# First attention: unscaled outputs divided by GpSimd with inverse sums sent through DRAM, and first steps placed between the picking rounds

## The chip, the cores and the metric

One core of one Trainium2 chip runs the whole program. The metric is the time of one execution on the device in microseconds (us). The engines are TensorE (PE in the profile; PEld is its weight load), VectorE (DVE), ScalarE (ACT), GpSimd (POOL) and SyncE (SP, which here only starts transfers). Each runs its own instruction stream in order, and the streams meet at semaphores.

## The reference, cut to what matters

The program computes two transformer blocks on 512 tokens of width 1024 in float32. The change touches the first mixer of the first block, an attention over the keys that an index score picks: 16 query heads of width 64, 4 key heads, 128 picked keys per query, causal.

```python
def block(i):                       # 128 queries
    ...
    s = einsum('bqhd,bsd->bqhs', iq_b, ik) * IDX_DIM ** -0.5
    score = einsum('bqh,bqhs->bqs', iw_b, relu(s))       # 8 index heads
    score = where(causal, score, -inf)
    _, sel = lax.top_k(score, top_k)                     # top_k = min(256, L // 4) = 128
    ...
    logits = einsum('bqgrd,bqkgd->bqgrk', q_b, k_sel) * A_HEAD_DIM ** -0.5
    logits = where(valid, logits, -inf)
    p = softmax(logits)
    o = einsum('bqgrk,bqkgd->bqgrd', p, v_sel)
...
mix = o @ w_o                       # then layer norm, MLP, and the other mixers
```

## The kernel before

Tokens are tiled in T = 4 tiles of 128. Every large product is done in three passes of fp32r matmuls: each operand is split into a high part (ACT's copy, `high`, line 1243) and a low part (the difference, `low`, DVE's line 1859), and high x high, high x low and low x high are summed. Weights come in numbered chunks of 1 MB: SP fetches chunk i into one of three `raw` buffers as soon as the low part of chunk i - 3 is made. For a few chunks (`pool_low` = 5, 6, 7, 8) POOL makes the low part (line 2772). Chunks 7 and 8 belong to the second half of the query projection, 9 to 12 to the output projection (`a_w_o`), 13 on to the MLP. Chunks 11 and 12 use slots that overlap buffers of the attention (`lent`), so ACT waits for the attention's last output before it writes them.

Before the attention, DVE picks the keys. For token tiles 1, 2 and 3 it runs 16 rounds each of `max` (the 8 largest, line 2214) and `match_replace` (line 2216), and then turns the result into a bias of 0 or -1e30 (line 2220). This runs as a job beside the projections of k, v and q on PE. Tile 0 needs no picking.

The attention (`attend` with key "A") is written out as a software pipeline of 32 units. Unit u is the pair of heads j = u // 4 and the query tile t = u % 4, and covers 128(t+1) keys; each unit has two score blocks i = 2u and 2u + 1, one per head. Step u of the pipeline does on

- PE: the scores of unit u (line 818); the transposes of the probabilities of unit u - 3 (line 827, `LAG`), and every second step the products with v (line 843), half 0 or 1 of the outputs of a pair, two units later still;
- DVE: for both blocks the biased scores and their maximum in one instruction (line 2097); for unit u - 1 the reciprocal of the row sum (line 2110) and, for t = 2 and 3, the scaling of the probabilities by it (line 2114); the copy of one transposed block out of its bank (line 2126); at the end of a pair the low part `xl` of the output (line 2229);
- ACT: both exponentials with row sums (line 1399); the copy of the other transposed block (line 1343); at the end of a pair the high part `xh` (line 1473);
- POOL: for t = 0 and 1 the scaling (line 2761).

PE's transposes therefore wait for scaled probabilities. PE's eight PSUM banks are handed out in turn, and each `take` waits until the bank's last reader is done. When the second query half is projected (`gemm_tok(("q", 1), ...)`), POOL rotates it (`rotary`, lines 2746 to 2750, with `gb` as scratch), and after step 3 PE transposes it (line 540, 16 transposes in four banks) and ACT copies it (line 1248).

After the attention `first_half` runs chunk 9 and then chunk 10 against the outputs of head pairs 0 to 3 (lines 720 to 722), and `cross` runs chunks 11 and 12 against pairs 4 to 7.

## Time and profile before

| | |
|---|---|
| median of 3 runs | 1945.25 us (1945.1 to 1946.36) |
| profiled execution | 1947.47 us, of which the span is 1945.5 us |
| PE busy | 1869.9 us (96%) |
| DVE busy | 1184.5 us (61%) |
| ACT busy | 734.1 us (38%) |
| POOL busy | 136.5 us (7%) |

The span in 40 slices of 48.6 us; a digit is the busy share in tenths, and PEclk is the granted clock in tenths. The first attention lies in the third to fifth slice.

```profile
PE   9989999999999999999999999789899899999997
DVE  4989676555556676577544546766775554333437
ACT  4447343232223434544222223535554352222221
POOL 0343000000000151000000000000230000000000
PEclk9989999999999999999999999989999899999998
```

Busy times are sums of instructions and say nothing of who waits for whom. A matmul's end is modelled, so short waits of PE are seen best from the starts of its groups. In the timeline a row is a start, a duration, the engine, the line, the operation with its operands and the number of merged instructions, and in brackets the idle time before it and what ended it.

### The profile page before, as it was taken

What the parts mean: (1) busy time and instruction counts of PE and PEld (TensorE: products, weight loads), DVE (VectorE), ACT (ScalarE), POOL (GpSimd) and SP (SyncE); (2) the same over time, 40 slices, a digit from 0 to 9 for tenths busy, and PEclk for the clock granted to TensorE, in tenths of its full rate; (3) what the DMA queues carried; (4) which work ended last, traced back from release to release, by engine and by line L of the source; (5) the groups of instructions that cost most, each with busy time, mean ns of one, the idle gap of its engine ahead of it and who ended that gap; (6) DMA issues with size and microseconds to landing.
All of it is one profiled execution on the core that took longest, in us unless ns stands there. A gap on an engine that the chain in (4) does not pass through costs nothing.

```text
span 1945.5 us, 23033 instructions
## 1 busy us (share of the span) xinstructions
PE 1869.9 (96%) x9172; PEld 1507.9 (78%) x9172; DVE 1184.5 (61%) x2191; ACT 734.1 (38%) x1146; POOL 136.5 (7%) x136
## 2 busy tenths in 40 slices
PE   9989999999999999999999999789899899999997
PEld 7765788878888888788888888677556698888885
DVE  4989676555556676577544546766775554333437
ACT  4447343232223434544222223535554352222221
POOL 0343000000000151000000000000230000000000
PEclk9989999999999999999999999989999899999998
DMA  6210425434442212234343342031001413323221
GB/s 203 66 65 2 152 84 167 161 130 138 144 149 70 74 57 66 66 108 134 127 130 108 118 142 88 23 109 44 1 1 60 146 33 99 108 87 108 87 87 44
DMA packets 116874, 184.04 MB, mean 95 GB/s; under 512 B 7152, under 2 KB 71792, under 8 KB 113696
## 3 DMA queue, kind: packets, MB, share of 16 engines
q1 hardware_dynamic: 115376, 177.77, 27.7%
q0 software_dynamic: 1392, 4.82, 0.9%
q8 instruction: 72, 1.18, 0.3%
q14 instruction: 34, 0.28, 0.0%
HBM read 180.47 MB, written 2.10 MB: 94 GB/s over the span
## 4 chain that ended last, share of the span: by engine, by line
PE 74%; DVE 17%; ACT 5%; issue 3%; POOL 1%; DMA 0%; SPq 0%; DVEq 0%; ACTq 0%
PE bank L593 10%; PE bank L595 10%; PE bank L594 10%; PE bank L784 7%; PE bank L786 7%; PE bank L785 7%; DVE wl L1859 2%; PE bank L567 2%; PE bank L569 2%; PE bank L568 2%; DVE gb L2216 2%; DVE m L2214 1%; PE bank L843 1%; PE bank L615 1%; PE bank L617 1%
## 5 line engine op out<-in xcount | busy, mean ns | idle before, releaser
L1859 DVE TENSOR_TENSOR wl<-raw,wh 128x2048 fp32r<-128x2048 f32 (+1 forms) x138 | 310.3, 2254 | 200.6 <-ACT wh L1243 200.3
L1243 ACT ACTIVATE wh<-raw 128x2048 fp32r<-128x2048 f32 (+1 forms) x142 | 265.2, 1883 | 244.4 <-PE bank L786 90.0
L593 PE MATMUL bank<-xh,wh 128*128 128x512 f32 (+2 forms) x880 | 348.1, 396 | 2.3 <-DVE wl L1859 2.3
L594 PE MATMUL bank<-xh,wl 128*128 128x512 f32 (+2 forms) x880 | 347.0, 394 | 0.0
L595 PE MATMUL bank<-xl,wh 128*128 128x512 f32 (+2 forms) x880 | 347.0, 394 | 0.0
L786 PE MATMUL bank<-wh,ul 128*128 128x512 f32 x592 | 230.4, 389 | 0.0
L785 PE MATMUL bank<-wl,uh 128*128 128x512 f32 x592 | 230.4, 389 | 0.0
L784 PE MATMUL bank<-wh,uh 128*128 128x512 f32 x592 | 230.4, 389 | 0.0
L593 PEld LDWEIGHTS bank<-xh,wh 128*128 128x128 f32 (+2 forms) x880 | 165.3, 188 | 43.0 <-DVE wl L1859 3.1
L595 PEld LDWEIGHTS bank<-xl,wh 128*128 128x128 f32 (+2 forms) x880 | 165.2, 188 | 38.8
L594 PEld LDWEIGHTS bank<-xh,wl 128*128 128x128 f32 (+2 forms) x880 | 165.4, 188 | 38.3
L2026 DVE TENSOR_TENSOR h<-h,bank 128x512 f32<-128x512 f32 x112 | 75.4, 684 | 105.0 <-PE bank L786 102.0
L1363 ACT ACTIVATE A<-bank 128x512 f32<-128x512 f32 x64 | 38.2, 597 | 258.2 <-PE bank L595 254.6
L567 PE MATMUL bank<-wh,xh 128*128 128x512 f32 (+1 forms) x320 | 126.9, 397 | 2.5 <-DVE wl L1859 2.5
L785 PEld LDWEIGHTS bank<-wl,uh 128*128 128x128 f32 x592 | 111.1, 188 | 23.3
L784 PEld LDWEIGHTS bank<-wh,uh 128*128 128x128 f32 x592 | 111.1, 188 | 23.2
L786 PEld LDWEIGHTS bank<-wh,ul 128*128 128x128 f32 x592 | 111.1, 188 | 23.2
L568 PE MATMUL bank<-wl,xh 128*128 128x512 f32 (+1 forms) x320 | 122.6, 383 | 0.0
L569 PE MATMUL bank<-wh,xl 128*128 128x512 f32 (+1 forms) x320 | 122.6, 383 | 0.0
L2035 DVE TENSOR_TENSOR A<-A 128x512 f32<-128x512 f32 x64 | 44.1, 690 | 93.7 <-ACT A L1363 93.5
L1343 ACT ACTIVATE A<-bank 128x512 f32<-128x512 f32 (+5 forms) x107 | 51.5, 491 | 96.2 <-PE bank L569 40.6
L695 PE MATMUL bank<-xh,wh 128*128 128x256 f32 x256 | 73.6, 287 | 0.9 <-DVE xl L1912 0.3
(363 smaller groups left out, 3102.9 us busy)
## 6 DMA issues: line engine op xcount, KB each, us to landing
raw<-in_mlp_w_up SPq DMA_DIRECT2D x32, 1024.0 KB, 5.6
raw<-in_mlp_w_down SPq DMA_DIRECT2D x32, 1024.0 KB, 5.1
raw<-in_w_ada SPq DMA_DIRECT2D x24, 1024.0 KB, 5.0
raw<-in_b_w_in SPq DMA_DIRECT2D x12, 1024.0 KB, 5.4
raw<-in_w_in SPq DMA_DIRECT2D x11, 1024.0 KB, 5.2
raw<-in_w_gate SPq DMA_DIRECT2D x11, 1024.0 KB, 5.3
raw<-in_w_up SPq DMA_DIRECT2D x11, 1024.0 KB, 5.4
raw<-in_w_down SPq DMA_DIRECT2D x10, 1024.0 KB, 5.0
```

What stands on the lines that cost most here:

```text
L567: pe.matmul(o, X, H[:, k, :], start=kk == 0, stop=False)
L568: pe.matmul(o, X, L[:, k, :], start=False, stop=False)
L569: step = pe.matmul(o, Y, H[:, k, :], start=False, stop=kk == 7)
L593: pe.matmul(o, H[:, k, c], xh[:, k, :], start=k == 0, stop=False)
L594: pe.matmul(o, L[:, k, c], xh[:, k, :], start=False, stop=False)
L595: step = pe.matmul(o, H[:, k, c], xl[:, k, :], start=False, stop=k == 7)
L784: pe.matmul(o, X, H[:, f, :], start=f == 0, stop=False)
L785: pe.matmul(o, X, L[:, f, :], start=False, stop=False)
L786: step = pe.matmul(o, Y, H[:, f, :], start=False, stop=f == nf - 1)
L1243: act.activation(slots[slot_of[i]][0][:, 0:n], raw[:, i % NRAW, 0:n], ACT.Copy).then_inc(*s_high.up(i))
L1859: dve.tensor_tensor(L[:, 0:n], raw[:, i % NRAW, 0:n], H[:, 0:n].bitcast(F), ALU.subtract).then_inc(*s_low.up(i))
L2026: dve.tensor_tensor(hv, hv, ps, ALU.add).then_inc(*s_row.up(name))
```

## The change

- DVE takes one reciprocal per head pair (8 columns: two heads, four tiles) and none per block; nobody scales the probabilities. PE's transposes wait for the exponentials alone, and `LAG` for this attention falls from 3 to 2.
- Per head pair PE transposes the 8 inverse columns to 8 rows (`turn_inverses`), DVE copies them to SBUF, SP stores them to DRAM (4 KB) and reads them back so that partitions 0 to 63 hold the row of one head and 64 to 127 that of the other (`spread`, two loads of 128 KB). SP does this after the fetch of chunk 12 and before that of chunk 13.
- ACT copies the unscaled output aside (`pl`), POOL multiplies it with the spread inverses, then ACT makes `xh` and DVE `xl` from it. These come five and six steps later than before, so the loops on ACT and DVE are six steps longer.
- The first three steps of the attention run earlier: on PE and ACT between token tiles of the last query projection, on DVE after picking rounds 11, 13 and 15 of tile 3. The transposes of the second query half come after step 4, counted from 0 (before: after step 3).
- The low part of chunk 9 goes from DVE to POOL. POOL's rotary scratch moves from `gb` to `pl`.
- ACT's high part of chunk 12 waits also for the low part of the last output.

```diff
-        pool_low = (5, 6, 7, 8)
+        pool_low = (5, 6, 7, 8, 9)
...
-        LAG = {"A": 3, "B": 2}
+        LAG = 2
+
+        inv = [tmp[:, i] for i in range(3)]
+        rows_inv = [tmp[0:8, 3, P * i:P * i + P] for i in range(4)]
...
# PE, turn_p
-                    w.wait_ge(*(s_pool if by_pool(key, i) else s_step).at((key, "norm", i)))
+                    if key == "A":
+                        w.wait_ge(*s_act.at((key, "exp", i)))
+                    else:
+                        w.wait_ge(*(s_pool if by_pool(i) else s_step).at((key, "norm", i)))
...
+                def turn_inverses(j):
+                    b = banks.take((key, "rcT", j))
+                    w.wait_ge(*banks.free((key, "rcT", j), s_act.sem))
+                    w.wait_ge(*s_step.at((key, "rc", j)))
+                    pe.transpose(bank[b][0:8, 0:P], att[:, 2, 2 * j:2 * j + 2, :].rearrange("p g t -> p (g t)"),
+                                 ident).then_inc(*s_turn.up((key, "rcT", j)))
...
                         turn_p(2 * g + 1)
+                        if key == "A" and g % T == T - 1:
+                            turn_inverses(g // T)
...
-            gemm_tok(("q", 1), 512, "x", 2)
-            drain(jobs)
...
+            gemm_tok(("q", 1), 512, "x", 2, after=lambda t: t and next(heads))
+            assert not jobs
+            for n, _ in enumerate(heads):
+                if n == 1:
                     turn(("qT", 1), tmp, 4, s_pool.at("rot q1"))
...
# ACT, high
                 if lent.get(i) == "o1":
                     w.wait_ge(*s_mm.at(("A", "o", 7, 1)))
+                    if slot_of[i] == 3:
+                        w.wait_ge(*s_xlow.at(("A", "o", 7)))
...
+            def divided(j):
+
+                w.wait_ge(*s_pool.at(("A", "div", j)))
+                act.activation(xh[:, j, :], pl[:, j], ACT.Copy).then_inc(*s_xhigh.up(("A", "o", j)))
...
+                    g = u - lag - 7
+                    if key == "A" and 0 <= g < N and g % T == T - 1:
+                        divided(g // T)
...
             def emit_a(j, ps):
-                act.activation(xh[:, j, :], ps, ACT.Copy).then_inc(*s_xhigh.up(("A", "o", j)))
+                w.wait_ge(*s_pool.at("rot q1"))
+                copy_to(("A", "un", j), pl[:, j], ps)
...
# DVE, attend
+                    if key == "A":
+                        if 0 <= g < N and g % T == T - 1:
+                            j = g // T
+                            w.wait_ge(*s_act.at((key, "exp", 2 * g + 1)))
+                            dve.reciprocal(rc[:, 2 * j:2 * j + 2, :], sm[:, 2 * j:2 * j + 2, :]).then_inc(*s_step.up((key, "rc", j)))
...
+                    g = u - lag - 1
+                    if key == "A" and 0 <= g < N and g % T == T - 1:
+                        j = g // T
+                        w.wait_ge(*s_turn.at((("qT", 1), 3)))
+                        w.wait_ge(*s_turn.at((key, "rcT", j)))
+                        if j > 3:
+                            w.wait_ge(s_sums, 16 * (j - 3))
+                        dve.tensor_copy(rows_inv[j % 4], bank[banks.of[key, "rcT", j]][0:8, 0:P]).then_inc(*s_step.up((key, "inv", j)))
+                        banks.read[key, "rcT", j] = s_step.at((key, "inv", j))
+                    g = u - lag - 8
+                    if key == "A" and 0 <= g < N and g % T == T - 1:
+                        j = g // T
+                        w.wait_ge(*s_xhigh.at((key, "o", j)))
+                        emit(j)
...
# DVE, top_k
+                        if t == T - 1 and r in (11, 13, 15):
+                            next(heads)
                         yield
...
# POOL
-            attend("A", PB1, 16, True)
+            for j in range(8):
+                w.wait_ge(*s_act.at(("A", "un", j)))
+                w.wait_ge(s_inv[j % 3], 32 * (j // 3 + 1))
+                pool.tensor_tensor(pl[:, j], pl[:, j], inv[j % 3], ALU.mult).then_inc(*s_pool.up(("A", "div", j)))
...
# SP
+            def spread(j):
+                w.wait_ge(*s_step.at(("A", "inv", j)))
+                sp.dma_start(sums[j].rearrange("g t q -> (g t) q"), rows_inv[j % 4]).then_inc(s_sums, 16)
+                w.wait_ge(s_sums, 16 * (j + 1))
+                if j > 2:
+                    w.wait_ge(*s_pool.at(("A", "div", j - 3)))
+                for p in range(2):
+                    sp.dma_start(inv[j % 3][64 * p:64 * p + 64, :], sums[j, p].rearrange("t q -> (t q)").partition_broadcast(64)).then_inc(s_inv[j % 3], 16)
...
                 fetch(i)
+                if i == mixed[0] + 3:
+                    for j in range(8):
+                        spread(j)
```

## Rows read from the trace of the kernel before

**Rows 1.** Windows: stretch, length, busy PE, PEld, DVE, ACT, POOL, granted clock, DMA.

```profile
126.40:133.00 6.60, 0.00 (x0) 0.01 (x1) 6.57 (x16) 1.77 (x8) 4.83 (x5) 0.68 0.34 110
133.00:139.00 6.00, 5.84 (x26) 4.88 (x26) 3.51 (x19) 5.34 (x18) 2.37 (x3) 0.50 0.15 56
...
149.60:191.90 42.30, 41.56 (x303) 24.56 (x301) 40.25 (x168) 32.61 (x106) 15.07 (x20) 1.00 0.01 2
191.90:202.40 10.50, 9.72 (x83) 6.54 (x81) 8.12 (x29) 6.67 (x19) 3.01 (x4) 1.00 0.01 2
```

**Rows 2.** Timeline of PE, start of the attention.

```profile
123.91 2.43 PE L818 MATMUL bank<-A 64*128 64x128 f32 x16
133.03 1.03 PE L827 MATMUL bank<-C,rz 128*128 128x128 f32 x2 [6.69 <-POOL rz L2761]
133.85 3.62 PE L540 MATMUL bank<-C,A 128*128 128x128 f32 x16
...
139.11 0.70 PE L818 MATMUL bank<-A 64*128 64x256 f32 x4
```

**Rows 3.** Timeline of DVE: first round of the last ranking, and what follows it.

```profile
102.07 0.59 DVE L2220 TENSOR_SCALAR A<-gb 128x384 f32<-128x384 f32 x1
102.58 0.68 DVE L2214 MAX8 m<-A 128x8 f32<-128x512 f32 x1
...
126.74 2.72 DVE L1859 TENSOR_TENSOR wl<-raw,wh 128x2048 fp32r<-128x2048 f32 x1
129.38 1.48 DVE L2220 TENSOR_SCALAR A<-gb 128x512 f32<-128x512 f32 x1
130.90 0.29 DVE L2097 CUSTOM_DVE_ANT_0 rz<-bank,A 128x128 f32<-128x128 f32 x1
```

**Rows 4.** Timeline of POOL in the same stretch.

```profile
105.29 4.61 POOL L2772 TENSOR_TENSOR wl<-raw,wh 128x2048 fp32r<-128x2048 f32 x1
124.69 1.26 POOL L2746 TENSOR_TENSOR gb<-A,rot 128x512 f32<-128x512 f32 x1 [14.79 <-ACT A L1343]
...
127.39 3.19 POOL L2750 TENSOR_TENSOR A<-gb 128x512 f32<-128x512 f32 x1
```

**Rows 5.** Timeline of PE through one head pair.

```profile
160.03 1.13 PE L818 MATMUL bank<-A 64*128 64x512 f32 x4
161.09 0.44 PE L827 MATMUL bank<-C,rz 128*128 128x128 f32 x2
161.55 0.49 PE L818 MATMUL bank<-A 64*128 64x128 f32 x4
...
164.22 0.70 PE L818 MATMUL bank<-A 64*128 64x256 f32 x4
164.85 0.87 PE L827 MATMUL bank<-C,rz 128*128 128x128 f32 x6
165.66 0.92 PE L818 MATMUL bank<-A 64*128 64x384 f32 x4
```

**Rows 6.** Groups by line and shape, 149.6 to 191.9 us: count, busy, mean ns.

```profile
L1399 ACT ACTIVATE rz<-rz,att 128x512 f32<-128x512 f32 x10 | 7.1, 716 | 1.9 <-DVE att L2097 1.9
...
L2114 DVE TENSOR_SCALAR rz<-rz,att 128x512 f32<-128x512 f32 x10 | 4.9, 487 | 0.4
```

**Rows 7.** Timeline after the attention: PE, DVE, ACT.

```profile
202.40 0.50 PE L720 MATMUL bank<-wh,xh 128*128 128x512 f32 x1
...
205.01 6.70 DVE L1859 TENSOR_TENSOR wl<-raw,wh 128x2048 fp32r<-128x2048 f32 x3 [1.18 <-ACT wh L1243]
...
213.67 1.92 ACT L1243 ACTIVATE wh<-raw 128x2048 fp32r<-128x2048 f32 x1 [5.14 <-PE bank L722]
```

**Rows 8.** DMA issues over the whole span: count, KB each, median us to landing.

```profile
out<-A SPq DMA_DIRECT2D x4, 512.0 KB, 2.6
...
gb<-in_ln_mix_g POOLq DMA_DIRECT2D x2, 512.0 KB, 3.9
...
C<-in_cst SPq DMA_DIRECT2D x1, 64.0 KB, 1.9
```

More of the change, by code:

```diff
@@ L351, in program @@
         bank = [ctx.enter_context(nc.psum_tensor(f"bank{i}", [P, 512], F)) for i in range(8)]
+        sums = nc.dram_tensor("sums", (8, 2, T, P), F, kind="Internal").ap()
         s_gemm = Signal(sem("s_gemm"))
@@ L372, in program @@
         s_gb = sem("s_gb")
+        s_sums = sem("s_sums")
+        s_inv = [sem(f"s_inv{i}") for i in range(3)]
         s_out = sem("s_out")
@@ L847, in outs @@
                         banks.drop((key, "o", j))
-                lag = LAG[key]
+                def turn_inverses(j):
[4 more added lines that the diff above has]
+                                 ident).then_inc(*s_turn.up((key, "rcT", j)))
+                lag = LAG
                 for u in range(N + lag + 3):
@@ L1249, in turned_to, with gemm_tok @@
                     banks.read[key, j] = s_act.at((key, j))
-            def gemm_tok(key, n, evict, ticks=0, last_ticks=None, first=None):
+            def gemm_tok(key, n, evict, ticks=0, last_ticks=None, first=None, after=None):
                 k0 = 0
@@ L1263, in gemm_tok @@
                             evict(t, bank[banks.of[key, t]][:, 0:n])
+                            if after:
+                                after(t)
                         tick(jobs, ticks)
@@ L1390, in attend @@
                 nmx, sm = att[:, 0, 0:nheads, :], att[:, 1, 0:nheads, :]
-                lag = LAG[key]
-                for u in range(N + lag + 3):
+                lag = LAG
+                for u in range(N + lag + (9 if key == "A" else 3)):
                     if u < N:
@@ L1468, in scalar_program @@
             jobs.append(later(("qT", 0), 4, qT[:, 0:4, :]))
-            gemm_tok(("q", 1), 512, lambda t, ps: copy_to((("q", 1), t), tmp[:, t, :], ps), 2)
-            drain(jobs)
             def emit_a(j, ps):
-                act.activation(xh[:, j, :], ps, ACT.Copy).then_inc(*s_xhigh.up(("A", "o", j)))
-            for n, _ in enumerate(attend("A", PB1, PT1, 16, True, emit_a, ())):
-                if n == 3:
+                w.wait_ge(*s_pool.at("rot q1"))
+                copy_to(("A", "un", j), pl[:, j], ps)
+                banks.read["A", "o", j] = s_act.at(("A", "un", j))
+            heads = attend("A", PB1, PT1, 16, True, emit_a, ())
+            gemm_tok(("q", 1), 512, lambda t, ps: copy_to((("q", 1), t), tmp[:, t, :], ps), 2, after=lambda t: t and next(heads))
+            assert not jobs
+            for n, _ in enumerate(heads):
+                if n == 1:
                     turned_to(("qT", 1), 4, qT[:, 4:8, :])
@@ L2082, in attend @@
                 nmx, sm, rc = (att[:, q, 0:nheads, :] for q in range(3))
-                lag = LAG[key]
-                for u in range(N + lag + 3):
+                lag = LAG
+                for u in range(N + lag + (9 if key == "A" else 3)):
                     if u < N:
@@ L2110, in attend @@
                             dve.reciprocal(rc[:, hd, t:t + 1], sm[:, hd, t:t + 1]).then_inc(*s_step.up((key, "rc", i)))
-                            if not by_pool(key, i):
+                            if not by_pool(i):
                                 pb = bufs[i % NB][:, 0:P * (t + 1) if causal else SEQ]
@@ L2130, in attend @@
                     g = u - lag - 2
-                    if 0 <= g < N and g % T == T - 1:
+                    if key == "B" and 0 <= g < N and g % T == T - 1:
                         j = g // T
@@ L2225, in vector_program @@
             gemm_tok(("q", 1), None, 2)
-            drain(jobs)
-            def emit_a(j, ps):
-                dve.tensor_tensor(xl[:, j, :], ps, xh[:, j, :].bitcast(F), ALU.subtract).then_inc(*s_xlow.up(("A", "o", j)))
-            for _ in attend("A", PB1, PT1, 16, True, emit_a, [s_pool.at("rot q1")]):
+            assert not jobs
+            for _ in heads:
                 pass
@@ L2755, in attend @@
                 for i in range(nheads * T):
-                    if not by_pool(key, i):
+                    if not by_pool(i):
                         continue
@@ L2783, in gpsimd_program @@
             low(8)
+            low(9)
             w.wait_ge(*s_act.at((("q", 1), T - 1)))
```

16 lines of the change are left out of this document (9 added, 7 removed).

## The prediction

> **What bounds the kernel now.** The granted-clock line of the page shows a kernel that is TensorE (PE) work almost everywhere (96% of 1945.5 us), so only stretches where PE stands still or runs at a lower clock can be won. I read first the windows around the first attention [rows 1]. Between 126.4 and 133.0 PE does nothing; from 133.0 to 139.0 it is busy at a granted clock of 0.50, the 1.2 GHz level; before and after it is at 1.00. Inside the attention (149.6 to 191.9, five head pairs) three engines are nearly full at once: PE 41.6 of 42.3 us, VectorE (DVE) 40.3, ScalarE (ACT) 32.6. That is the point of this case: the change empties DVE, but PE has only 0.7 us of idle there.
>
> To see whether PE's fullness is real and not queueing, I took one pair by PE's own starts [rows 5]. From the scores of the widest query block (160.03) each group begins as the previous one streams out: 1.06, 0.46, 2.67 (scores, transposes and one output product), 0.63, 0.81 us and so on. Only the 0.46 varies between pairs (0.37 to 0.67): a wait for a bank. The rest repeats to 0.02 us. So a pair is about 8.2 us of PE work, whatever DVE does, and 8.4 with waits.
>
> Then the start of the attention, by engine. PE ends the projection with the scores of four units at 123.91 and cannot go on, since the first maxima are late: it resumes at 133.03, and reaches the scores of unit 5 at 139.11 [rows 2]. DVE is what it waits for [rows 3]: the last ranking (16 rounds from 102.58) is followed at 126.74 by the low half of chunk 9 (2.72), at 129.38 by the bias (1.48), and only at 130.90 by the first maximum.
>
> **The change part by part.** I follow the path to two marks: U5, the start of unit 5's scores (139.11), and E, the first matmul of the output projection (202.40 [rows 7]).
>
> *Start.* A ranking round is (126.74 - 102.58)/16 = 1.51 us, so round 11 ends at 120.7. Unit 0 (two maxima at 0.21 apart, plus a wait, 0.5) is slipped in there, unit 1 (0.8) after round 13, unit 2 (1.05) after round 15: the ranking now ends at 128.0, unit 2's maxima at 129.1, one 0.2 us copy follows, 129.3. Scores are there in time: PE ends its four token tiles before 123.91, each 12 matmuls of 0.23 = 2.7 us (0.23 as below), so the second near 118.4, and spends 1.3 us on scores between them. The low of chunk 9 (2.72) is gone from DVE; on GpSimd (POOL) it takes 4.6 as its neighbours do, inside the 14.8 us that POOL stood idle before 124.69 [rows 4]. Bias: 1.48 as measured, or about 0.7 if nothing is beside it (0.59 for 384 columns [rows 3]), so it ends between 130.0 and 130.8. Unit 3's first maximum is done at 130.7 to 131.5 (0.7). ACT then runs two exponentials at 0.72 [rows 6] and one short copy (0.27), which frees the bank of the third query transpose: 132.5 to 133.3. PE's last eight of the 16 query transposes (0.11 each, and 0.2 to switch) give U5 = 133.6 to 134.4. POOL's rotation of the second query half is no later: ACT evicts the last tile at about 125.9, behind an exponential; four operations end 4.0 us later at 130.5, or 132.4 if the last takes 3.19 again [rows 4]. I take 134.0, in the middle, since both overlaps can recur in part: **5.1 us won**. PE is then idle or waiting some 2.5 us between 128.0 and 133.4 in pieces of at most 1.1; the clock fell before when PE had stood for some 2.4 us (0.68 over 6.6 us is 2.4 at full and 4.2 at half), so I count full clock.
>
> On the bias the Trainium skill (page "SBUF — State Buffer", section "Who interferes with whom") says that a DVE instruction in a two-port mode and a GpSimd instruction exclude one another for a whole instruction. The pair 1.48 and 3.19 agrees with it. By that rule U5 would be 134.4 if the last rotation meets the bias, 133.6 if it doesn't.
>
> *Steady part.* Removed: 32 DVE scalings (0.49 us for the widest [rows 6]), 32 POOL scalings, 56 of 64 reciprocals. DVE falls from 8.05 to about 5.7 us a pair (40.25/5 less 1.8 of scalings and 1.05 of reciprocals, plus 0.2 and 0.3 for one wide reciprocal and an 8-row copy). ACT gets one more 128x512 activation (a plain copy, below the 0.72 of an exponential of that size [rows 6]): 6.5 to 7.1. POOL falls from 3.0 to one product of 1.3. All stay under PE's 8.2, so DVE's 2.4 us are covered by PE and worth nothing by themselves. What remains: PE's waits between U5 and E, 0.74 in five pairs, 0.78 in the last stretch [rows 1]; I take 1.0 of these 1.5 as gone, bounds 0 and 1.5. The smaller lag means that at U5 one more transposing unit is done (0.81 [rows 5]). Added to PE: eight turns of inverses, 0.15 each (one transpose of 0.11 and part of a switch between kinds of matmul; bounds 0.11 and 0.3), 1.2 in all (0.9 to 2.4). The shorter lag doesn't starve PE: between the scores of a widest block and its transposes lie now 2.67 + 0.81 + 0.63 = 4.1 us of PE work, and two maxima and exponentials need about 2.7.
>
> So E = 134.0 + (202.4 - 139.1) - 0.8 - 1.0 + 1.2 = 196.7, **5.7 us earlier**.
>
> *The round trip.* DVE writes inverse rows, SyncE (SP) sends them to DRAM and reads them back to 128 partitions, POOL multiplies. The trace has no such small pair. The nearest rows: a 512 KB store 2.6, a 512 KB broadcast load on POOL's queue 3.9, a 64 KB load 1.9 [rows 8]. So the two in a row cost between 3.8 and 6.5. With 1.3 for the product the division is done 7 to 8 us after the rows, and ACT asks for it six steps (12 us) later: covered in the steady part,. SP's fetches behind the eight round trips (chunk 13 on) wait for DVE's low of chunk 10, which comes after the attention anyway.
>
> *The end.* Here the round trip is open. The last rows leave DVE about 1.5 us before E; then 5.3 (DMA, the middle), 1.4 (POOL), 0.7 (ACT), 0.8 (DVE): the low part of head pair 7 is ready near E + 6.5. ACT's high of chunk 10 is queued behind its copy, 1.9, and DVE's low 2.3: ready near E + 10. PE runs the 48 matmuls of chunk 9 without either, until about 213.4 before (ACT's wait for the end of them is over at 213.67 [rows 7]): 11.0 us, or 0.23 a matmul. Now ACT begins chunk 10 at E + 0.6 and DVE ends its three lows at E + 9.3 [rows 7], so there was slack. I take a stall of 0.2; bounds 0 and 2.
>
> Sum: 5.7 - 0.2 = 5.5 off the profiled span of 1945.5, and off the median of 1945.25 (the profiled execution's own time, 1947.47, holds 2 us outside the span): **1939.7 us**.
>
> **Rivals.** (a) *The clock falls again.* The pieces of idle before U5 come close enough; then the transposes and the first units run at the 1.2 GHz level as at [rows 2], where 16 transposes took 3.6 instead of 1.9. Price 1.7 to 3.5: 1942. For: 2.5 us of waiting in 5.4. Against: no piece over 1.1.
> (b) *ACT becomes the bound.* 7.1 of 8.2 us in strict order, now with a wait for POOL in its queue, behind which exponentials stand, and for those DVE and PE. If it sets a pair at 8.6, 7 x 0.3 are lost: 1942.
> (c) *The round trip decides the end: slower than before.* Place: chunk 10's halves on ACT and DVE, behind head pair 7. Every us of DMA beyond about 6.5 goes to PE one for one; to lose more than the 5.5 won and 3.9 more it must take 16 us. For: no row shows a store to DRAM that is read back at once. Against: the queue is empty then, and each half of the trip has a row under 4. Should each pair's trip exceed 10, ACT would block in every pair as well, and 12 would be enough. 1950 or more.
> (d) *More is won:* bias alone at 0.7, all waits gone, and no stall: 1938.4; with the short clock drops further on (the page's line shows them in the last third) falling otherwise by one or two, 1936.
>
> **Numbers.** Changes of 0.2% (3.9 us) are about what can be told from none. Forecast 1938.5 to 1941: 0.47; (d) 0.16; (a) 0.14, half of it within 0.2%; (b) and a stall of 2 or more at the end 0.15, mostly within 0.2%; (c) 0.08. Faster 0.69, same 0.22, slower 0.09. Range 1936 to 1944.5, which leaves out the slower case and the ends.
>
> **What would show it.** Right: PE's idle after 126 is broken into pieces, clock 1.00 from 126 to 139, unit 5's scores at 134, first output matmul near 197; a pair still 8.2 to 8.4 us with DVE down to 5.7; POOL's product 7 to 8 us after the rows; no gap at chunk 10. Wrong: a granted clock of 0.5 before 140, pairs of 8.6 with ACT full, or a PE gap 11 us after E.

## The result, and the profile after

Over 20 runs each, run by turns, the kernel takes 1939.41 us (median; 1934.14 to 1944.13) against 1944.63 before (1940.77 to 1946.39). The ratio is 0.9974, with a 95% interval of 0.9965 to 0.9982: 5.2 us or 0.27% faster. The forecast was 1939.7, the range 1936 to 1944.5. The profiled execution took 1942.17 us with a span of 1940.4.

The page of the kernel after, its engine line and the granted clock in slices (columns as before):

```profile
PE 1869.4 (96%) x9180; PEld 1506.2 (78%) x9180; DVE 1168.7 (60%) x2110; ACT 737.5 (38%) x1154; POOL 127.6 (7%) x113
...
PEclk9999999999999999999999999899999899999998
```

The third digit of the clock was 8 and is 9, that of PE likewise: the hole in the third slice is gone. The windows of the kernel after, for the stretches of [rows 1] where both ends still mean the same, and two for the end (length, busy PE, PEld, DVE, ACT, POOL, granted clock, DMA):

```profile
126.40:133.00 6.60, 5.24 (x36) 3.37 (x35) 5.88 (x21) 4.05 (x16) 4.10 (x4) 1.00 0.01 2
133.00:139.00 6.00, 5.91 (x42) 3.17 (x40) 3.56 (x14) 5.33 (x16) 0.00 (x0) 1.00 0.00 0
149.60:191.90 42.30, 41.86 (x306) 24.62 (x305) 31.95 (x116) 34.85 (x111) 6.40 (x5) 1.00 0.10 31
196.00:206.90 10.90, 10.90 (x49) 8.96 (x49) 4.78 (x4) 6.97 (x6) 2.49 (x3) 1.00 0.37 120
206.90:217.80 10.90, 10.90 (x50) 9.03 (x49) 6.79 (x4) 2.05 (x2) 0.00 (x0) 1.00 0.93 303
```

From 126.4 to 133.0 PE works 5.24 of 6.60 us where it did nothing, and the clock, which had been 0.68 and then 0.50, stays at 1.00. In the steady part DVE falls from 40.25 to 31.95 us and PE rises by 0.30. The output projection shows no gap in either of its chunks.

The two marks. Timeline of PE of the kernel after, start of the attention and first matmul of the output projection (start, duration, engine, line, operation, count, and in brackets the idle time before it):

```profile
118.83 0.49 PE L827 MATMUL bank<-A 64*128 64x128 f32 x4
...
129.27 0.49 PE L827 MATMUL bank<-A 64*128 64x128 f32 x4 [0.54 <-DVE att L2134]
130.20 0.87 PE L839 MATMUL bank<-C,rz 128*128 128x128 f32 x6 [0.44 <-ACT A L1369]
130.93 1.06 PE L549 MATMUL bank<-C,A 128*128 128x128 f32 x8
132.38 1.09 PE L549 MATMUL bank<-C,A 128*128 128x128 f32 x8 [0.38 <-ACT A L1369]
133.40 0.70 PE L827 MATMUL bank<-A 64*128 64x256 f32 x4
...
195.81 0.50 PE L729 MATMUL bank<-wh,xh 128*128 128x512 f32 x1
```

Unit 5's scores start at 133.40 (139.11 before [rows 2]; 134.0 predicted), the output projection at 195.81 (202.40 before [rows 7]; 196.7 predicted): 6.6 us earlier. The chain from here on is PE and the same instructions. By windows the stretch from 220 to 1215 is alike in both kernels, and the later stretches differ in granted clock by up to 0.01 (from 1215 to 1345 it is 0.92 before and 0.91 after, with PE busy for 111.18 and 109.89 us).

That is where 1.5 of the 6.6 us went in this one execution: in the second block's stages the clock falls for 3.4 us at a time, five times from 1231 to 1313 in the kernel before, and in the one after four times from 1222 to 1308, of which two lasted 6.8. Those drops fall differently from run to run. Over the 20 runs of the kernel after, the time follows the run's mean granted clock (1944.13 us at 0.982, 1934.14 at 0.987; correlation -0.89). So 1.5 us given back in one profile, and 1.4 by the medians, is within what these drops do to any run, and I don't put it down to the change. For the experiments this means: whole times can tell kernels apart by some 2 us only with many runs, and what the change does must be read at the mark E.

### The profile page after: what moved, and what is told of

It is laid out like the page before. It is cut to its first block, busy times and chain, and to the rows that moved or that the text cites. A ratio compares the mean times of both kernels' runs of the same rounds, so it can differ in the third digit from the quotient of the medians.

```text
span 1940.4 us, 22966 instructions
## 1 busy us (share of the span) xinstructions
PE 1869.4 (96%) x9180; PEld 1506.2 (78%) x9180; DVE 1168.7 (60%) x2110; ACT 737.5 (38%) x1154; POOL 127.6 (7%) x113
## 4 chain that ended last, share of the span: by engine, by line
PE 76%; DVE 16%; ACT 5%; issue 3%; POOL 0%; DMA 0%; DVEq 0%; ACTq 0%
PE bank L602 10%; PE bank L603 10%; PE bank L604 10%; PE bank L794 7%; PE bank L795 7%; PE bank L793 7%; DVE wl L1896 2%; PE bank L576 2%; PE bank L578 2%; PE bank L577 2%; PE bank L855 2%; PE bank L839 2%; DVE gb L2272 2%; DVE m L2270 1%; PE bank L827 1%
```

## The experiments

The stage itself starts earlier or later from one execution to the next. So I read E less the point T1 at which PE has done two of the four token tiles of the last projection: the first early scores where there are any (118.83 above), or, without early steps, the start of the first scores less two tiles of 2.72 us (123.91 [rows 2] less 5.44 is 118.47). T1 lies between 118.05 and 119.43 in the fourteen traces, and DVE moves with it: the first round of the last ranking starts 15.9 us before T1 in the kernel before (102.58) and in the one after (102.95). That this distance holds still shows in the kernels that should not differ: after and the one with the lengthened trip have 76.98 and 77.01; up to unit 5's scores, after and the one with the early row copy have 14.57 and 14.59.

| kernel | E | E - T1 | one head pair | half clock near the start | median us (runs) |
|---|---|---|---|---|---|
| before | 202.40 | 83.93 | 8.41 | 10.2 us | 1944.63 (20) |
| before + low 9 on POOL | 198.85 | 80.77 | 8.41 | 6.8 us | 1939.88 (11) |
| before + early steps | 202.81 | 83.38 | 8.41 | 6.8 us | 1946.85 (1) |
| before + both | 201.15 | 82.20 | 8.41 | 6.8 us | 1944.28 (10) |
| unscaled outputs alone | 201.42 | 82.92 | 8.48 | 6.8 us | 1940.74 (1) |
| unscaled + low 9 on POOL | 197.63 | 79.24 | 8.48 | 3.4 us | 1939.45 (5) |
| unscaled + early steps | 200.22 | 82.17 | 8.48 | 6.8 us | 1941.23 (10) |
| after (all three) | 195.81 | 76.98 | 8.48 | none | 1939.41 (20) |
| after, row copy early | 195.14 | 75.89 | 8.32 | none | 1934.94 (6) |
| after, lag 3 | 201.10 | 82.65 | 9.38 | none | 1940.52 (1) |
| after, lag 3, row copy early | 194.51 | 76.31 | 8.33 | none | 1936.8 (1) |
| after, trip with five stores | 196.28 | 77.01 | 8.48 | none (10.2 at 210) | 1945.77 (1) |
| after, DVE load added | 202.26 | 83.11 | 9.23 | none | 1946.39 (1) |
| row copy early, DVE load added | 199.15 | 80.74 | 8.60 (mean) | none | 1940.22 (1) |

The medians come from four series and compare only roughly with one another. Each series has its own runs of the kernel before: 20 runs at 1944.63 beside the kernel after; 24 at 1944.5 beside low 9 on POOL, unscaled + low 9, unscaled + early steps and the early row copy; 13 at 1942.66 beside the kernel with both, lag 3, the five stores and the first added load; and one at 1942.60 beside the last four experiments (the unscaled outputs alone, the early steps alone, the second load, and lag 3 with the early copy). A single run (1) tells nothing by its whole time; it is read at E.

### The three edits of the start, alone and in pairs

The low part of chunk 9 on POOL, alone, in the kernel before:

```diff
-        pool_low = (5, 6, 7, 8)
+        pool_low = (5, 6, 7, 8, 9)
...
             low(8)
+            low(9)
```

> The kernel before, with one edit alone: the low part of chunk 9 made by POOL instead of DVE. Theory: the start of the attention is DVE's chain, and 2.7 us of it are this one instruction, another 1.0 the bias instruction that it pushes beside POOL's last rotation (1.48 instead of 0.42). First maximum at 127.3 instead of 130.9; start of unit 5's scores at 135.6 if the clock still falls (PE then stands 3.2 us), near 134.5 if not; first output matmul near 199; total 3.5 to 4.5 us under before. Rival: the early steps of the attention are what pays, and this edit gives 1 us or less, with unit 5 at 138 or later.

Measured: 3.16 us earlier (80.77 against 83.93), ratio 0.9983 (0.9974 to 0.9992). PE and POOL of this kernel at the start:

```profile
123.52 2.43 PE L818 MATMUL bank<-A 64*128 64x128 f32 x16
129.36 1.03 PE L827 MATMUL bank<-C,rz 128*128 128x128 f32 x2 [3.41 <-POOL rz L2761]
130.19 3.62 PE L540 MATMUL bank<-C,A 128*128 128x128 f32 x16
...
127.00 1.33 POOL L2750 TENSOR_TENSOR A<-gb 128x512 f32<-128x512 f32 x1
```

One constant and one call give nearly half of the whole gain (3.16 of 6.95): DVE reaches its first maximum 3.7 us sooner. PE still stands for 3.41 us, waiting for POOL's scalings, and the 16 query transposes still run at the half clock (3.62 us as in [rows 2]).

The early steps without and with that, scaling kept (both kernels; the second has the edit above as well; the first three steps between token tiles and after picking rounds 11, 13 and 15, the transposes of the second query half after step 3, counted from 0):

```diff
-            gemm_tok(("q", 1), 512, "x", 2)
-            drain(jobs)
+            gemm_tok(("q", 1), 512, "x", 2, after=lambda t: t and next(heads))
+            assert not jobs
...
-                if n == 3:
+                if n == 0:
...
+                        if t == T - 1 and r in (11, 13, 15):
+                            next(heads)
```

> The kernel before with the early steps alone: chunk 9's low part on DVE, probabilities scaled, lag 3. Theory: PE waits for POOL's scalings behind its rotation, and the rotation is longer beside DVE's low part (3.2 instead of 1.3); first transposes at 133 or later, E - T1 84 to 86, no gain or a loss. Rival: the steps alone shorten DVE's chain and E - T1 is 82 or less.

> The kernel before, with two edits alone: the low part of chunk 9 on POOL, and the early steps. The probabilities are still scaled on DVE and POOL, the lag is 3, and nothing goes through DRAM. It asks what the title of the change is worth beside its two side edits. I count from T1, where PE has done two of the four tiles of the last projection: E - T1 was 83.9 us before, 77.0 after, 75.9 in the run with the early copy. Theory: at the start PE now waits for POOL, whose scalings of units 0 and 1 stand behind its rotation of the second query half (ended near 130.5): first transposes near 131, a clock fall likely, unit 5 near 136; E - T1 79.5 to 81, so 3 to 4.5 of the 7 us come without the title's part. Rival: the scaling costs nothing at the start either, and E - T1 is 77 to 78.

Measured: alone 0.55 us won (83.38, where 84 to 86 was expected); on top of low 9 they lose 1.43 (80.77 to 82.20, where 79.5 to 81 was expected). The whole time of the kernel with both can't be told from that of the kernel before: ratio 0.9999 (0.9987 to 1.0011). POOL and PE of the kernel with both:

```profile
129.41 1.54 POOL L2757 TENSOR_TENSOR A<-gb 128x512 f32<-128x512 f32 x1
130.93 3.35 POOL L2768 TENSOR_SCALAR rz<-rz,att 128x128 f32<-128x128 f32 x4
...
131.68 0.44 PE L827 MATMUL bank<-C,rz 128*128 128x128 f32 x1 [4.00 <-POOL rz L2768]
```

The early steps put scores into the projection, so its last tile and with it POOL's rotation end 2.6 us later (at 130.93 against 128.33; 1.7 of it if the later start of the stage, 0.87, is taken off), and the scalings of the first units stand behind the rotation in POOL's stream. PE waits 4.00 us for them in one piece. The early maxima are there and nobody can use them.

The unscaled outputs without the early steps, with and without low 9, and the kernel after without low 9:

```diff
-            gemm_tok(("q", 1), 512, "x", 2, after=lambda t: t and next(heads))
-            assert not jobs
-            for n, _ in enumerate(heads):
-                if n == 1:
+            gemm_tok(("q", 1), 512, "x", 2)
+            drain(jobs)
+            for n, _ in enumerate(heads):
+                if n == 4:
...
-                        if t == T - 1 and r in (11, 13, 15):
-                            next(heads)
```

> The kernel after, without the early steps: the first three steps of the attention come after the projection and after the last ranking, the rest as it is. Theory: on DVE the same instructions stand in another order, so unit 3's maxima end at the same time within 0.5 us and unit 5's scores start at 133.4 to 134.2; what changes is that PE stands about 2.5 us in one piece near 127 to 129, and the clock may fall then (1.7 to 3 us more). Without a fall the total is within 1 us of after. Rival: the early steps carry the gain, unit 5 starts 3 us later at 136 or more with the clock at its upper level.

> The kernel after without its two side edits: no early steps, and chunk 9's low part on DVE; what is left is the title of the change (unscaled outputs, round trip, lag 2). With it and the next run all eight combinations of the three edits but the bare one are measured. E - T1 so far: before 83.9; low part alone 80.8; low part and early steps 82.2; title and low part 79.2; title and early steps 82.2; all 77.0. Theory: DVE's chain (2.7 of low part, 1.5 of bias) sets the start, the clock falls as before, and what the title saves at the start is a reciprocal and scaling of 1 us: 82 to 83.5. Rival: the title alone carries the start: 80 or less.

```diff
-        pool_low = (5, 6, 7, 8, 9)
+        pool_low = (5, 6, 7, 8)
...
-            low(9)
```

> The kernel after, with the low part of chunk 9 given back to DVE. Theory: DVE's chain grows by 2.3 to 2.7 us, and by 1 more if the bias meets POOL's rotation again: unit 5's scores start at 136 to 137 instead of 133.4, the first output matmul is at 198.5 to 199.5, the total 2.7 to 3.5 us above after; the granted clock may fall to its lower level before 140, which would add up to 2 more. Rival: the early steps cover it, and unit 5 starts before 134.5.

Measured: unscaled outputs alone win 1.01, with low 9 4.69, with the early steps 1.76; their medians stand to the kernel before at 0.9972 (0.996 to 0.9984) with low 9 and at 0.999 (0.9979 to 1.0001) with the early steps. PE with low 9, then DVE and PE with the early steps:

```profile
128.51 0.62 PE L839 MATMUL bank<-C,rz 128*128 128x128 f32 x2 [3.11 <-ACT rz L1430]
129.07 1.60 PE L827 MATMUL bank<-A 64*128 64x512 f32 x4
```

```profile
128.48 2.28 DVE L1896 TENSOR_TENSOR wl<-raw,wh 128x2048 fp32r<-128x2048 f32 x1
130.68 1.49 DVE L2278 TENSOR_SCALAR A<-gb 128x512 f32<-128x512 f32 x1
...
133.07 3.79 PE L549 MATMUL bank<-C,A 128*128 128x128 f32 x16 [2.75 <-DVE att L2134]
```

Without early steps PE stands 3.11 us for the first exponentials, since the first maxima come only after the bias; without low 9 it stands 2.75 us for unit 3's, which come after the low part and the bias. In both the clock falls (scores of 512 keys take 1.60 instead of 1.13 us, 16 transposes 3.79 instead of some 1.8, by 0.11 each).

The three edits by themselves add up to 3.16 + 0.55 + 1.01 = 4.7 us; together they give 6.95. Each takes away one of three things that stand in a row before PE's second piece of work (DVE's queue, the order of the maxima, POOL's scalings), and only with all three gone does PE's idle time fall into pieces short enough for the clock to stay up. Beside low 9, the early steps lose 1.4 us where the probabilities are scaled and win 2.3 where they are not.

### The steady part: which bank PE waits for

One head pair, kernel after, PE (the products with v left out) and DVE:

```profile
145.66 1.13 PE L827 MATMUL bank<-A 64*128 64x512 f32 x4
146.88 0.66 PE L839 MATMUL bank<-C,rz 128*128 128x128 f32 x4
...
163.51 0.27 DVE L2185 COPY A<-bank 8x128 f32<-8x128 f32 x1
```

Between the widest scores and the transposes behind them lie 1.22 us where the same work took 1.06 [rows 5], in every pair (the DVE row is of a later pair, where these transposes start at 163.84, 0.06 after the copy in L2185 ends). What ends the wait in the groups by line is DVE's copy of the inverse rows (L2185): the bank that holds them is handed out again for these transposes. The rival was that the wait comes from ACT, or from the exponentials. The test is to let DVE copy the rows in the same step in which PE turns them, one step earlier:

```diff
-                    g = u - lag - 1
+                    g = u - lag
                     if key == "A" and 0 <= g < N and g % T == T - 1:
                         j = g // T
                         w.wait_ge(*s_turn.at((("qT", 1), 3)))
```

> The kernel after the change, with DVE's copy of the 8 inverse rows made one pipeline step earlier (in the step in which PE turns them) instead of one step later. In the kernel after, PE waits 0.16 us in every head pair at the transposes that follow the widest scores, and goes on 0.05 us after that copy ends. Theory: those transposes take the bank that the turned inverses held, which DVE frees late. Then the 0.16 is gone: a pair takes 8.32 us instead of 8.48, the start of unit 5's scores stays at 133.4, the first output matmul moves from 195.8 to about 194.7, and the total is 1.1 us less than after (about 1938.3 as a median). Rival: the wait belongs to another bank (ACT's copy of a transposed block); then a pair stays at 8.48 and nothing moves.

Measured: 8.32 us a pair instead of 8.48, E - T1 75.89 instead of 76.98, and the median is 1934.94 us (1932.42 to 1938.81), 0.9956 of the kernel before (0.9941 to 0.997). Timeline and window of this kernel:

```profile
162.58 1.13 PE L827 MATMUL bank<-A 64*128 64x512 f32 x4
163.64 0.66 PE L839 MATMUL bank<-C,rz 128*128 128x128 f32 x4
...
133.84:195.14 61.30, 61.30 (x458) 36.80 (x457) 44.17 (x158) 50.05 (x155) 8.93 (x7) 1.00 0.09 32
```

The gap is 1.06 again, and PE is busy for all 61.30 us from unit 5's scores to E. It shows how much PE work there is: 61.30 us. The kernel after took 62.41, so it waited 1.11. **This version is clearly faster than the kernel before, and 1.1 us ahead of the kernel after at the mark.** The medians lie 4.5 us apart, more than the mark explains; they are of two series, the intervals of the two ratios touch, and the mean granted clock here is 0.986 to 0.989, against 0.982 to 0.988. So I don't put the rest down to the edit.

How the lag bears on this:

```diff
-        LAG = 2
+        LAG = {"A": 3, "B": 2}
```

> The kernel after with the lag of the transposes back at 3 units. The prediction gave the shorter lag 0.8 us, one unit of transposes that PE does while it waits for DVE at the start. Theory: E - T1 grows from 77.0 to 77.8. Rival: the wait of 0.16 a pair at the bank of the turned inverses goes or grows with the order, and moves E - T1 by more than that either way (75.9 to 79).

> The kernel after with the lag at 3 and the early copy of the inverse rows. With lag 3 alone a pair took 9.39 us and PE waited 1.06 in each at the scores after the widest ones. Theory: that is the bank of the turned inverses again, whose copy DVE made behind the widest maxima. Then with the early copy the 1.06 is gone, a pair takes 8.3 to 8.45, and E - T1 is 76.5 to 77.5 (75.9 with lag 2). Rival: the lag itself costs it; then pairs stay above 9.

Measured: with lag 3 a pair takes 9.38 us; with lag 3 and the early copy 8.33, and E - T1 is 76.31. The first lies far outside both its expectation (77.8) and its rival (up to 79): E - T1 is 82.65. PE and DVE of the kernel with lag 3 alone:

```profile
168.04 0.66 PE L839 MATMUL bank<-C,rz 128*128 128x128 f32 x4 [1.00 <-DVE A L2185]
...
167.72 0.27 DVE L2185 COPY A<-bank 8x128 f32<-8x128 f32 x1
```

The copy now stands behind the widest maxima on DVE, and PE waits 1.00 us for its bank in every pair. So the shorter lag is worth 5.7 us where the copy is late, and 0.42 (76.31 less 75.89) where the copy is early. It was not the exponentials that needed it.

### What DVE's relief is worth

The load that the change took from DVE was put back as results that nobody uses: for each block a reciprocal, and for 384 and 512 keys a scaling into a spare buffer. In the first kernel both reciprocals of a unit write beside each other with a wait for the one before; in the second (shown), on top of the early row copy, only the scalings wait.

```diff
+                        if 0 <= g < N:
+                            for i in (2 * g, 2 * g + 1):
+                                ...
+                                dve.reciprocal(small[:, 320 + i:321 + i], sm[:, hd, g % T:g % T + 1]).then_inc(*s_step.up())
+                                if g % T > 1:
+                                    n = P * (g % T + 1)
+                                    w.wait_ge(*s_step.now())
+                                    dve.tensor_scalar(pl[:, 7, 0:n], bufs[i % NB][:, 0:n], 0.5, None, ALU.mult).then_inc(*s_step.up())
```

> The kernel after, with DVE's old load put back as work that nobody uses: a reciprocal per block, and for the tiles 2 and 3 a scaling of the block into a spare buffer. Theory: DVE's relief is worth little by itself, since PE's 8.3 us bind a pair; DVE goes from 6.4 to about 8.2 us a pair. A pair stays within 8.5 to 8.7 (the copy of the inverse rows comes later, and PE's wait before the transposes that follow the widest scores grows from 0.16 to at most 0.4), E - T1 grows from 77.0 by 1 to 2. Rival: DVE was the bound of before; then a pair takes 8.8 or more and E - T1 grows by 3 or more.

> The kernel after with the early copy of the inverse rows, and DVE's old load put back as unused work in the form in which before had it (reciprocals without waits between them, each scaling behind its reciprocal). The run with the load alone gave pairs of 9.0 to 9.2 us, against my 8.5 to 8.7; its load was some 0.8 us a pair too large, through waits between its small reciprocals. It tells whether DVE's time or the bank of the inverse rows was the cause. Theory now: both engines were level before (8.2 each), so DVE's own time decides as soon as anything is added; with about 8.3 to 8.5 us of instructions DVE binds, a pair takes 8.5 to 8.7 and PE idles 0.2 to 0.4 in each; against 8.32 with the early copy and no load. Rival: it was the bank; then a pair stays at 8.32 to 8.4 with the load.

Measured: 9.23 us a pair for the first, more than the 8.5 to 8.7 of its expectation and past the 8.8 of its rival; 8.60 in the mean of six pairs for the second, within its 8.5 to 8.7. Windows of the first, then of the second:

```profile
149.60:191.90 42.30, 38.95 (x289) 23.47 (x291) 38.13 (x162) 33.09 (x102) 5.91 (x5) 1.00 0.10 33
```

```profile
149.60:191.90 42.30, 40.80 (x301) 23.88 (x297) 41.44 (x171) 33.62 (x107) 6.85 (x5) 1.00 0.10 32
```

The first is no clean measure of DVE's load. DVE is busy for less time (38.13) than in the kernel before (40.25) and yet a pair is longer: it stands idle for 3.0 us in this window before its own small reciprocals, through waits that I had put in, and PE waits some 0.8 us in every pair for the copy of the inverse rows, which comes later behind them. Load and bank are mixed.

The second is cleaner, and its mean hides two kinds of pairs. From one start of the widest scores to the next they take 8.27, 8.32, 8.95, 8.88, 8.33 and 8.83 us. In those of 8.32 and 8.33 PE loses nothing against the kernel without the load (8.32), although DVE is busy for 8.19 us of the latter. In each of the three long ones an added scaling, which takes 0.43 by itself (the next one, at 161.31), meets POOL's product and takes 1.32 to 1.43. POOL, DVE and PE in the first long pair:

```profile
159.65 1.27 POOL L2858 TENSOR_TENSOR pl<-pl,A 128x512 f32<-128x512 f32 x1 [4.82 <-ACT pl L1369]
159.77 1.43 DVE L2155 TENSOR_SCALAR pl<-rz 128x512 f32<-128x512 f32 x1
...
164.20 1.13 PE L827 MATMUL bank<-A 64*128 64x512 f32 x4 [0.56 <-ACT A L1369]
```

The lengthened scaling ends 0.28 us after the product. Against the same kernel without the load E - T1 grows by 4.85 us: 1.19 before unit 5's scores, where the bias meets POOL's last rotation and takes 1.37 instead of 0.42; 0.69 from there to the first widest scores; 1.66 in the six pairs; and 1.31 at the end, where one more scaling (194.91, 1.36) meets a product. So the rival, that the waits are all the bank's and the load is free, falls. But what the load costs is mostly its meetings with POOL and not DVE's time as such. This split is read from one trace; a load that keeps out of POOL's way was not run.

### The round trip, lengthened

```diff
-                            w.wait_ge(s_sums, 16 * (j - 3))
+                            w.wait_ge(s_sums, 80 * (j - 3))
...
-                sp.dma_start(sums[j].rearrange("g t q -> (g t) q"), rows_inv[j % 4]).then_inc(s_sums, 16)
-                w.wait_ge(s_sums, 16 * (j + 1))
+                for n in range(5):
+                    sp.dma_start(sums[j].rearrange("g t q -> (g t) q"), rows_inv[j % 4]).then_inc(s_sums, 16)
+                    w.wait_ge(s_sums, 16 * (5 * j + n + 1))
```

> The kernel after, with the round trip made longer: the store to DRAM is made five times, each waited for, where one such store takes 1.2 us from its issue to the next step, so 4.9 us more. Theory: inside the attention nothing changes (a pair 8.48: the quotient is asked for 12 us after the rows and ready after 11). At the end the low part of chunk 10 was ready 9.9 us after the first output matmul, and PE needs it at 10.95; so 1.0 of the 4.9 is hidden and PE stands 3.9 us at its 145th output matmul. Rival: ACT, which waits for POOL in order, holds up exponentials as well, and pairs take 9 us or more.

The last trip of the kernel after, first, then of this one (SPq is SP's queue; a row of it is the time in which it issues):

```profile
194.52 0.27 DVE L2185 COPY A<-bank 8x128 f32<-8x128 f32 x1
...
194.82 0.27 SPq L2899 DMA_DIRECT2D sums<-A  x1
196.02 1.19 SPq L2904 DMA_DIRECT2D A<-sums  x2
...
199.63 1.30 POOL L2849 TENSOR_TENSOR pl<-pl,A 128x512 f32<-128x512 f32 x1 [3.90 <-DMA A<-sums]
...
203.51 6.70 DVE L1896 TENSOR_TENSOR wl<-raw,wh 128x2048 fp32r<-128x2048 f32 x3 [1.18 <-ACT wh L1267]
```

```profile
194.99 0.27 DVE L2185 COPY A<-bank 8x128 f32<-8x128 f32 x1
...
195.83 1.69 SPq L2905 DMA_DIRECT2D A<-sums  x2
197.57 6.08 SPq L2900 DMA_DIRECT2D sums<-A  x5
204.58 1.09 SPq L2905 DMA_DIRECT2D A<-sums  x2
...
208.27 1.26 POOL L2849 TENSOR_TENSOR pl<-pl,A 128x512 f32<-128x512 f32 x1 [6.93 <-DMA A<-sums]
...
214.44 0.79 PE L729 MATMUL bank<-wh,xh 128*128 128x512 f32 x1 [6.97 <-DVE wl L1896]
```

Inside the attention nothing changes (E - T1 77.01, 8.48 a pair): there the trip is covered, as long as it stays below a pair. At the end the division comes 8.2 us later against E (8.64 by the rows, less 0.47 of a later E). Four more stores of 1.2 would be 4.8, but the five took 7.0 (1.4 each), and SP took them up only at 197.57, 2.3 us after the rows were ready, since it was still at the trip before. PE has its 48th matmul out at 207.31 and stands for 7.1 us (6.97 by the row), ahead of the first matmul of chunk 10, the 49th of the output projection (the expectation names a wrong number for it). 8.17 of delay less 7.13 of stall leave **1.0 us of slack** at the end of the kernel after. The clock is at the half level for 10.2 us from 209.9 on, so that the 13 matmuls from 214.44 take 5.7 us where 13 of 0.227 take 2.95. The rival (c) has the place that the prediction named. Its price is higher than one for one, by 2.7 us of slow clock, and it decides from a last trip of 5.9 us on (4.8 measured and 1.0 of slack), where the prediction had about 6.5.

## Why the prediction was right, and where it was not

**The bound, and PE alone.** Right. Only two things were to be won, the hole at the start and PE's waits. With DVE's busy time down by 8.3 us in five pairs, a pair by PE's starts is 8.48 us, above the 8.41 of before.

**Start: 5.1 us predicted, 6.1 measured** (unit 5's scores less T1, 20.64 before and 14.57 after). Against the start of the last ranking, the bias began 0.4 us sooner than predicted (26.3 us after it and not 26.7). The chain went by the steps named: unit 2's maxima to 129.04, copy, bias, unit 3's maximum, copy, transposes. DVE of the kernel after:

```profile
129.04 0.29 DVE L2168 COPY gb<-bank 128x128 f32<-128x128 f32 x1
129.24 0.42 DVE L2278 TENSOR_SCALAR A<-gb 128x512 f32<-128x512 f32 x1
129.80 0.69 DVE L2134 CUSTOM_DVE_ANT_0 rz<-bank,A 128x512 f32<-128x512 f32 x1
```

The term that was off most is the bias: bounds 0.7 and 1.48, measured 0.42, outside both. The lower bound was taken from the 0.59 for 384 columns [rows 3] as if that were undisturbed. In the trace of before a POOL rotation (101.15, 1.29) runs beside it; the nearer row was a scaling of 512 columns, 0.49 [rows 6]. The same instruction took 0.73 in the kernel with low 9 alone and 1.49 without low 9, and the traces say why: in the kernel before the rotation (127.39, 3.19) ends at 130.58 and the bias at 130.86; with low 9 alone POOL's third operation ends at 126.92 and the bias at 127.20; without low 9 the rotation ends at 131.88 and the bias at 132.17. Each time the bias ends 0.28 or 0.29 us after the POOL instruction that was running when it was due. In the kernel after it was first, and the rotation beside it took 1.48, against 1.33 with low 9 alone. In the same way the last rotation takes 3.19 in the kernel before and 3.33 without low 9, because DVE's low part started just before it: it ends 1.12 us behind that low part in both. The Trainium skill (page "SBUF — State Buffer", section "Who interferes with whom") says that whoever issues first holds the shared pair for the whole instruction, and that a DVE instruction with two SBUF inputs shuts out POOL's reads. These rows agree. The prediction used it for a range of two ends; read as a rule of order it says which end: a bias that is due just ahead of the last rotation isn't held up, and a rotation with no low part ahead of it isn't either. The prediction had read the 1.48 and the 3.19 as one pair that lengthened each other; by the rows above the 3.19 belongs to DVE's low part of chunk 9, which the change takes away. And the 0.42 hangs on little, which was luck for the forecast: the bias began 0.07 us before the rotation (0.07 and 0.08 in the kernels with the early row copy and with the five stores). In the kernel with the load and the early row copy it came 0.18 us behind the rotation (129.08 and 128.90) and took 1.37, which the prediction's upper bound covers.

**The clock.** Right: 1.00 from 126 to 139 (windows above). PE's waiting there was 1.36 us, where the prediction had some 2.5, in three pieces of at most 0.54. Rival (a) didn't come in this kernel; it came in every kernel of the table whose PE stood in one piece for 2.75 us or more near the start, and in none whose longest piece there was 1.2 us or less. The two kernels with the load waited 2.2 us in pieces of at most 1.06 and kept the full clock.

**The lag, 0.8; waits, 1.0; turned inverses, 1.2.** From unit 5's scores to E 63.29 us became 62.41, that is 0.88 won where 0.6 was predicted. By parts: PE's work is 61.30 (above). The extra unit transposed before the mark took 0.81 away, as predicted; over the whole distance from T1 the shorter lag is worth less, 0.42 by the two kernels with the early copy. The turned inverses cost 0.11 each, since from the transposes before to the products behind lie 0.93 and 0.20 us, and the second is the switch that was there anyhow: 0.9 for eight, against 1.2 with bounds of 0.9 and 2.4. So 61.23 of the 63.29 were work before, and the waits fell from 2.06 to 1.11: 0.95 gone against 1.0. The sum was right, its picture was not: what remains is no rest of the old waits but a new one, 0.16 us in every pair, made by the change's own row copy.

**"Worth nothing by itself".** DVE's 2.4 us "are covered by PE and worth nothing by themselves": for DVE's own time this holds. PE is the bound of the kernel after, and with the load put back on top of the early row copy the pairs without a meeting take 8.32 and 8.33 us, as without it. It is too strong for the scalings: left in, they meet the product that the change gives to POOL, and such pairs take 8.83 to 8.95. The prediction priced such a meeting for the bias alone. DVE's busy time itself was 6.4 us a pair and not 5.7: I took the full durations of the removed instructions off a busy time in which neighbours overlap (a maximum of 0.69 starts at 129.80 and its reading at 130.42).

**ACT as the bound (b).** Didn't come: 34.85 us in five pairs is 7.0 a pair (7.1 predicted), and with the row copy early PE never waits.

**The round trip.** Predicted 3.8 to 6.5 between rows and product, 5.3 taken; measured 4.67 from the issue of the store in the pair at 146.85, and 4.81 in the last one (194.82 to 199.63). The store took 1.2 us to the next issue, less than half of the 2.6 of its nearest row [rows 8]; the two loads about 3.5. The division is done 6.1 us after the rows (194.79 to 200.93), not 7 to 8, which took the upper half of the range.

**The end.** The low part of chunk 10 was predicted at E + 10 and needed at E + 11. The first of the three lows that begin at 203.51 ends near 205.8, E + 10.0, and PE takes it up with its 49th matmul at 206.87, E + 11.06. The stall of 0.2 didn't come, and the slack by these rows, 1.1, is the 1.0 of the lengthened trip.

**The time.** The sum gave 1940.0 for the span, and it was 1940.4: an E that was 0.9 us better than predicted, and clock drops near 1240 and 1301 that gave 1.5 back. The agreement to 0.3 us in the median is partly luck, also because the forecast started from a median of 1945.25 (3 runs), which became 1944.63 with 20: 5.5 us were predicted and 5.2 measured. The steps were each within 1 us.

**Left open.** Whether the early row copy can be combined with still earlier first steps was not tried. Which of PE's idle stretches make the clock fall is known only by the traces here, and the length of one piece doesn't decide it. Near the start of the attention pieces of up to 1.2 us passed and single ones of 2.75 us and more brought a fall. Later on, a piece of 1.65 us (before 280.84, kernel after) passed and one of 2.12 (before 1908.61) had a fall with it; one of 2.77 (before 1286.06) passed in the kernel after, while one of 2.76 at the same place (before 1291.71) brought a fall in the kernel before.

## What to carry to other kernels

When several engines feed the first work of a pipeline, edits that each take away one of the waits in a row are not worth their single gains: here 3.2, 0.6 and 1.0 us alone, 6.95 together, and one pair of them was worse than one alone. Cost them on the chain that is left after the others. When PE is the bound and hands out banks in turn, every small new PSUM result is a new reader in that chain, and its copy must be placed ahead of long instructions: moving one 8-row copy one step ahead was worth 1.1 us at the mark with a lag of 2 and 6.3 with a lag of 3, and all but 0.4 of the 5.7 that looked like the worth of the shorter lag. And read a mean over pairs pair by pair: 8.60 here was 8.3 without and 8.9 with a meeting of two engines.

## What the runs showed of the hardware

- A DVE instruction of 128x512 that took 0.42 us in the kernel after took 0.58 to 1.49 in others beside POOL's, each time ending 0.28 to 0.29 us after the POOL instruction that had begun before it; POOL's 1.3 us rotation took 3.19 to 3.39 where a DVE subtraction of two SBUF operands had begun at most 0.65 us before it, and ended 1.12 us after it.
- A 4 KB store to DRAM on SP's queue was done 1.2 us after its issue (1.4 when five follow each other), and two broadcast loads of 128 KB from there reached their user 3.4 to 3.7 us after the first issue. The whole trip cost 4.7 to 4.8 us.
- PE's clock stayed at 2.4 GHz through 1.36 us of idle time in 6.6 (kernel after) and through 2.2 us in pieces of at most 1.06 (kernels with the load), and fell to 1.2 GHz during or behind single pieces of 2.1 to 7 us, for 3.4 to 10.2 us. A piece of 2.77 us (kernel after, before 1286.06) brought no fall.
